# One stream of projection blocks through three stages, with the next stage's first weights prepared ahead

## The reference

```python
proj = xn @ w_in[l]   # [branch gates (3*D) | RWKV-7 cols | S5 cols | Mamba-2 cols (z, xBC, dt)]
o_r = ...             # RWKV-7 time mixing
o_s = ...             # S5: Re(C h) + D u, with the scan h of a diagonal complex state
o_m = ...             # Mamba-2 SSD
merged = sig(g_r)*o_r + sig(g_s)*o_s + sig(g_m)*o_m
out = merged @ w_out[l]
# then cross-attention into 256 memory tokens (keys and values from RMSNorm(mem)), and an MLP
```

## Time and profile before

| | |
|---|---|
| median of 3 runs | 4519.31 us (4514.93 to 4529.73) |
| profiled execution | 4515.67 us |
| its span | 4513.9 us |
| TensorE busy over the span | 4102.0 us (91%) |
| VectorE, ScalarE, GpSimd busy | 2517.0, 1420.3, 222.7 us |

### The profile page before, as it was taken

How to read it: one execution, slowest core, us unless ns; L and a number is a source line. 1 busy time by engine, 2 the same in 40 slices (tenths; PEclk the granted TensorE clock), 3 DMA queues, 4 the chain that set the end, 5 groups by cost and what they waited for, 6 DMA issues and landing times. The chain is left out here.

```text
span 4513.9 us, 84409 instructions
## 1 busy us (share of the span) xinstructions
PE 4102.0 (91%) x35797; PEld 3747.0 (83%) x35797; DVE 2517.0 (56%) x4994; ACT 1420.3 (31%) x2428; POOL 222.7 (5%) x161
## 2 busy tenths in 40 slices
PE   8789999989989999878886999987998899999998
PEld 4779989989978888777885777776977889999997
DVE  3334646431278885258766877765553255444446
ACT  2112222221167553322103444433531252111112
POOL 0000000000001111022110000000001100000000
PEclk9899999989989999988997999998999999999999
DMA  5222222233355554545541100005222221111112
GB/s 186 77 84 83 89 82 88 69 98 112 104 146 142 159 145 123 155 141 163 176 141 40 32 29 31 32 13 174 92 96 89 74 90 61 47 47 47 39 37 77
DMA packets 374261, 418.68 MB, mean 93 GB/s; under 512 B 49162, under 2 KB 315964, under 8 KB 373020
## 3 DMA queue, kind: packets, MB, share of 16 engines
q1 hardware_dynamic: 361599, 368.01, 26.8%
q0 software_dynamic: 7680, 27.97, 2.1%
q10 hardware_dynamic: 4608, 17.30, 1.0%
HBM read 289.10 MB, written 121.77 MB: 91 GB/s over the span
## 5 line engine op out<-in xcount | busy, mean ns | idle before, releaser
L1718 PE MATMUL bank<-sum_x_hi,sum_w_hi 128*128 128x352 f32 x768 | 262.8, 342 | 95.4 <-DVE sum_x_lo L1701 38.0
L210 PE MATMUL bank<-xn_hi,pz_whi 128*128 128x352 f32 (+1 forms) x984 | 328.2, 334 | 21.0 <-DVE pz_wlo L195 14.9
L210 PE MATMUL bank<-xn_hi,pz_wlo 128*128 128x352 f32 (+1 forms) x984 | 319.7, 325 | 0.0
L210 PE MATMUL bank<-xn_lo,pz_whi 128*128 128x352 f32 (+1 forms) x984 | 318.0, 323 | 0.0
L3071 PE MATMUL bank<-bx_hi,bp_whi 128*128 128x384 f32 (+1 forms) x768 | 273.8, 357 | 29.7 <-DVE bx_lo L3129 18.4
L224 ACT ACTIVATE ring<-bank 128x352 f32<-128x352 f32 (+1 forms) x273 | 125.6, 461 | 536.0 <-PE bank L210 535.6
L210 PE MATMUL bank<-xn_hi,pb_whi 128*128 128x352 f32 x816 | 274.9, 337 | 18.9 <-DVE pb_wlo L195 13.0
L210 PE MATMUL bank<-xn_lo,pb_whi 128*128 128x352 f32 x816 | 266.1, 326 | 0.0
L210 PE MATMUL bank<-xn_hi,pb_wlo 128*128 128x352 f32 x816 | 265.2, 325 | 0.0
L1718 PE MATMUL bank<-sum_x_lo,sum_w_hi 128*128 128x352 f32 x768 | 256.5, 334 | 0.0
L1718 PE MATMUL bank<-sum_x_hi,sum_w_lo 128*128 128x352 f32 x768 | 256.3, 334 | 0.0
(11 more groups left out here) (695 smaller groups left out, 12227.7 us busy)
## 6 DMA issues: line engine op xcount, KB each, us to landing
ring<-in_w_in_dram SPq DMA_DIRECT2D x90, 512.0 KB, 4.9
proj_scratch<-ring SPq DMA_DIRECT2D x66, 528.0 KB, 3.0
m_seg<-acum_scratch SPq DMA_DIRECT2D x32, 512.0 KB, 7.0
ring<-in_mlp_w_dram SPq DMA_DIRECT2D x16, 1024.0 KB, 5.6
ring<-in_mlp_w_dram SPq DMA_DIRECT2D x32, 512.0 KB, 3.5
gates_scratch<-ring SPq DMA_DIRECT2D x24, 528.0 KB, 4.7
merged_scratch<-sum_gate ACTq DMA_DIRECT2D x24, 528.0 KB, 5.7
m_raw<-proj_scratch SPq DMA_DIRECT2D x24, 512.0 KB, 5.5
```

The source lines that it names most:

```text
L210: last = self.nc.tensor.matmul(ps[0:n, 0:m], w[:, q, 0:n], self.pair[x][:, q, t0:t0 + m], start=q == 0 and j == 0, stop=q == KD - 1 and j ...
L1718: last = self.nc.tensor.matmul(self.banks[e % n][:, 0:m], w[:, b % 2, q, :], self.pair[x][:, q, t0:t0 + m], start=q == 0 and i == 0, stop= ...
```

## The change

- **One stream.** `Columns` is built once, with 91 blocks and two more after them (`follow`): the first two blocks of the output products' weights. Its semaphores are kept over the stages' ends, and its split buffers (`pw_whi`, `pw_wlo`) live until `Sums` is done, which uses them too; the first half of `S5Input` keeps four of its eight row tiles there. Each stage loads two blocks beyond its own last and splits one. The stage of the S5 input loads the first two.
- **Stores.** A stage other than the last no longer waits for its last blocks' stores; the second stage waits for them at its start.
- **Drains.** `used` is gone in `Columns` and `Sums`: ScalarE waits for the product count. In `S5Input` the last matmul of each row tile counts.
- **S5 input.** The prompt products are stored before the sample product is awaited. The first half's eight loads are issued in `front`; the value store goes behind them.
- **S5 weights.** The two halves of a kernel product are issued alternately, and the second writes partitions 64 to 79.
- **Output products.** Block 0 comes split, block 1's weights come loaded. The first input chunk is loaded and split in two halves, and inputs are loaded before weights.

The core of the diff:

```diff
 class Columns:
...
+    def __init__(self, k, pair, parts, follow, split, banks):
+        self.k, self.nc, self.pair, self.banks = k, k.nc, pair, banks
+        self.blocks = [b for part in parts for b in part]
+        self.edges = [sum(len(part) for part in parts[:i]) for i in range(len(parts) + 1)]
+        self.W = [b[0] for b in self.blocks] + follow
...
         n = 2 * KD * P
...
+    def fetch(self, sp, b):
+        sp.dma_start(self.raw[:, b % 2, :, 0:self.width(b)], self.W[b].rearrange("(t p) n -> p t n", p=P)).then_inc(self.loaded[b % 2], 16)
...
     def load(self, sp):
-        for b, (W, _, _) in enumerate(self.blocks):
+
+        for b in range(self.first + 2, self.last + 2):
             yield self.at(b - 2, 0.2)
-            if b >= 2:
-                sp.wait_ge(self.w_lo, b - 1)
-            sp.dma_start(self.raw[:, b % 2, :, 0:self.width(b)], W.rearrange("(t p) n -> p t n", p=P)).then_inc(self.loaded[b % 2], 16)
+            sp.wait_ge(self.w_lo, b - 1)
+            self.fetch(sp, b)
+
+    def prime_load(self, sp, us, freed, count):
+
+        yield us
+        sp.wait_ge(freed, count)
+        for b in range(2):
+            self.fetch(sp, b)
+
+    def settle(self, sp, b):
...
+        for s in range(2):
+            sp.wait_ge(self.stored[s], 16 * ((b + 1 - s) // 2))
+
+    def settled(self, sp):
+
+        yield -100
+        self.settle(sp, self.first)
 
     def store(self, sp):
-        for b, (_, dst, _) in enumerate(self.blocks):
+        for b in range(self.first, self.last):
             yield self.at(b + 1, 0.4)
             sp.wait_ge(self.off, 3 * (b + 1))
-            sp.dma_start(dst, self.staging[0:self.width(b), b % 2, :]).then_inc(self.stored[b % 2], 16)
...
-            sp.wait_ge(self.stored[s], 16 * ((len(self.blocks) + 1 - s) // 2))
+            sp.dma_start(self.blocks[b][1], self.staging[0:self.width(b), b % 2, :]).then_inc(self.stored[b % 2], 16)
+        if self.last == len(self.blocks):
+            yield self.at(self.last + 2)
+            self.settle(sp, self.last)
 
...
     def high(self, act):
-        for b in range(len(self.blocks)):
-            yield self.at(b - 1, 0.5)
+        for b in range(self.first + 1 if self.first else 0, self.last + 1):
+            yield self.at(b - 1, 0.5) if b else -50
             act.wait_ge(self.loaded[b % 2], 16 * (b // 2 + 1))
             if b >= 2:
-                act.wait_ge(self.used, b - 1)
+                act.wait_ge(self.product, 3 * (b - 1))
             n = self.width(b)
...
@@ -210,11 +245,10 @@
                         last = self.nc.tensor.matmul(ps[0:n, 0:m], w[:, q, 0:n], self.pair[x][:, q, t0:t0 + m],
                                                      start=q == 0 and j == 0, stop=q == KD - 1 and j == 2)
                 last.then_inc(self.product, 1)
-            pe.drain().then_inc(self.used, 1)
 
...
 class S5Input:
...
     def sync(self, sp):
...
-                sp.dma_start(self.raw[:, s, q, :], self.k.w_in[q * P:(q + 1) * P, C_S + s * 512:C_S + (s + 1) * 512]).then_inc(self.loaded[s], 16)
+        for q in range(KD):
...
             yield self.at(s, Q5 + 2)
+            sp.wait_ge(self.off, 9 * s + Q5)
+            sp.dma_start(self.k.u_dram[:, 4 * s:4 * s + 4, :], self.out[:, :].rearrange("p (z n) -> p z n", z=4)).then_inc(self.stored, 16)
             sp.wait_ge(self.off, 9 * (s + 1))
-            sp.dma_start(self.k.u_dram[:, 4 * s:4 * s + 4, :], self.out[:, :].rearrange("p (z n) -> p z n", z=4)).then_inc(self.stored, 16)
...
-                        last = self.nc.tensor.matmul(self.banks[n % 6][0:rows, :], self.pair[x][:, q, at], w[:, q, :],
+                        last = self.nc.tensor.matmul(self.banks[n % 6][0:rows, :], self.pair[x][:, q, at], w[q],
                                                      start=q == 0 and j == 0, stop=q == KD - 1 and j == 2)
-                    if i == Q5 and s == 0:
-                        pe.drain().then_inc(self.freed, 1)
+                    if i == Q5 and s == 0 and q < KD - 1:
+                        last.then_inc(self.freed, 1)
...
                 for q in range(QP):
                     last = nc.tensor.transpose(bank[:, q * P:(q + 1) * P], v.ab[:, ri, q].rearrange("p t c -> p (t c)"), k.ident[:, :])
                 last.then_inc(self.turned, 1)
-            for half in range(2):
-                yield self.at(z, -0.40 + 0.05 * half)
-                pe.wait_ge(self.made_c, z + 1)
-                pe.wait_ge(self.off, 2 * z + 2)
-                if half:
-                    pe.wait_ge(self.kern_off, 2 * z + 1)
-                at = slice(64 * half, 64 * half + 64)
-                for q in range(QP):
-                    for ri in range(2):
-                        last = nc.tensor.matmul(bank[0:GC, q * P:(q + 1) * P], v.bb[at, ri, q0 + q, :],
+            yield self.at(z, -0.40)
+            pe.wait_ge(self.made_c, z + 1)
+            pe.wait_ge(self.off, 2 * z + 2)
+            for q in range(QP):
+                for ri in range(2):
+                    for half in range(2):
+                        at = slice(64 * half, 64 * half + 64)
+                        last = nc.tensor.matmul(bank[64 * half:64 * half + GC, q * P:(q + 1) * P], v.bb[at, ri, q0 + q, :],
                                                 v.ca[at, s, ri, q, 0:8, :].rearrange("p t c -> p (t c)"), start=ri == 0, stop=ri == 1)
-                last.then_inc(self.turned, 1)
+            last.then_inc(self.turned, 2)
 
...
                 act.wait_ge(self.turned, 4 * z + 3 + half)
                 if z and half == 0:
                     act.wait_ge(self.placed[1 - s], 16 * Q5 * ((z + 1) // 2))
-                activation(v.kern[:, half:ZG:2, :], bank[0:GC, :].rearrange("p (q n) -> p q n", q=QP), ACT.Copy).then_inc(self.kern_off, 1)
+                activation(v.kern[:, half:ZG:2, :], bank[64 * half:64 * half + GC, :].rearrange("p (q n) -> p q n", q=QP), ACT.Copy).then_inc(self.kern_off, 1)
...
 
             @block.tensor
...
-            if b >= 2:
-                sp.wait_ge(self.w_lo, b - 1)
-            sp.dma_start(self.raw[:, b % 2, :, :], j.W.rearrange("(t p) n -> p t n", p=P)).then_inc(self.loaded[b % 2], 16)
+            if b < 2:
+                continue
+            yield self.at(b - 2, 0.2)
+            if b >= 3:
+                sp.wait_ge(self.w_lo, b - 2)
+            sp.dma_start(self.raw[:, self.slot(b), :, :], j.W.rearrange("(t p) n -> p t n", p=P)).then_inc(self.loaded[b % 2], 16)
...
-                sp.dma_start(self.xraw[:, e % 2, :, :], src[:, :, t0:t0 + m]).then_inc(self.x_in[e % 2], 16)
+                if e == 0:
+                    sp.dma_start(self.xraw[:, 0, 0:4, :], src[:, 0:4, t0:t0 + m]).then_inc(self.early_in, 16)
+                q0 = 0 if e else 4
+                sp.dma_start(self.xraw[:, e % 2, q0:, :], src[:, q0:, t0:t0 + m]).then_inc(self.x_in[e % 2], 16)
...
             yield self.at(b - 1, 0.5)
-            act.wait_ge(self.loaded[b % 2], 16 * (b // 2 + 1))
-            if b >= 2:
-                act.wait_ge(self.used, b - 1)
...
+            if b == 1:
+                act.wait_ge(self.columns.loaded[s], 16 * ((self.base + 1) // 2 + 1))
+            else:
+                act.wait_ge(self.loaded[b % 2], 16 * (b // 2))
...
@@ -1707,18 +1768,21 @@
             for c, (t0, m) in enumerate(chunks3()):
...
-                    pe.wait_ge(self.w_lo, b + 1)
-                if b == self.first[j.x]:
+                if c == 0 and b:
+                    pe.wait_ge(self.w_lo, b)
+                if e == 0:
+                    pe.wait_ge(self.early_lo, 1)
+                elif b == self.first[j.x]:
...
                 for q in range(KD):
+                    if e == 0 and q == 4:
+                        pe.wait_ge(self.x_lo, 1)
...
-            pe.drain().then_inc(self.used, 1)
 
...
-                weave(sums.weights(sp), sums.load_x(sp), sums.previous(sp), sums.gates(sp))
+                weave(sums.load_x(sp), sums.weights(sp), sums.previous(sp), sums.gates(sp))
...
@@ -4057,12 +4126,16 @@
             W = w["xa_wk" if n < 2 else "xa_wv"][0]
             sp.dma_start(self.raw[:, n % 2, :, :], W[:, (n % 2) * 512:(n % 2 + 1) * 512].rearrange("(t p) n -> p t n", p=P)).then_inc(self.loaded[n % 2], 16)
         for v, name in enumerate(("mem_k_prompt", "mem_v_prompt")):
+            if v:
+                yield self.START[3] + 4
+                sp.wait_ge(self.k_off, 4)
+                sp.dma_start(self.k.key_dram, self.keyT[:, :, :]).then_inc(self.out, 16)
+                sp.wait_ge(self.product, 6)
+                for q in range(KD):
+                    sp.dma_start(self.raw[:, 0, q, :], self.k.w_in[q * P:(q + 1) * P, C_S:C_S + 512]).then_inc(self.k.s5_first, 16)
             yield (self.START[2], self.START[3] + 16)[v] + 2
             sp.wait_ge(self.p_off, 4 * (v + 1))
             sp.dma_start(o[name][0, 0].rearrange("(a p) h d -> p a (h d)", p=P), self.made[v][:, :, :]).then_inc(self.out, 16)
-        yield self.START[3] + 20
```

(35 more changed lines are left out.)

129 lines of the change are left out of this document (77 added, 52 removed).

## The result

The changed kernel takes 4424.15 us (median of 4 runs, 4419.95 to 4426.89), the kernel before 4523.39 us (4514.93 to 4529.73). The ratio is 0.9781, with a 95% interval of 0.9768 to 0.9793: faster by 99 us, where 4434 us was forecast in a range of 4416 to 4466. The two profiled executions lie closer together: 4515.67 and 4426.89, 88.8 us apart, since that of before was 7.7 us under its median and that of after 2.7 us over its own.

The account below looks back on a forecast made before the run. TensorE was taken to bound the three projection stages, with waits limiting the output products. The terms sum to −83.5 us from the profiled 4515.67, that is 4432; with part of the base's 3.6 us, forecast 4434, range 4416 to 4466.

Parts of the forecast that it names:

- Drains: Block ends: removing drains saves 16 us in the first stage, 6 second, 12.5 third, 5 output products, 2.1 S5 input.
- the forecast's 12.5: Third projection stage, 34 block ends: 12.5 us saved by removing drains, reduced from 14.3 for waits on others.
- the first rival: Later stages: TensorE waits for the second stream instead, only the first stage's drain gain remains, 4459 us; chance 0.15.
- the 10 us at which the prediction was to fall: Third stage: the forecast falls if TensorE's waits for VectorE or ScalarE rise by more than 10 us.
- Kernel products: S5 weights: alternating halves lets two passes start in the time of one, saving 14 us, bounds 0 and 15.
- The first stage: First projection stage, 41 blocks: shorter by 30 us, from 16 for drains and 14 for S5 kernel products.
- The front: Memory keys to S5 input: stage opens 8.3 us later, parameters give back 6; net +2.4, bounds −2 and +4.5.
- first S5 product later than 140: Start of the S5 input products: a sign that the prediction is wrong, if the first one starts after 140 us.
- Boundaries: Four stage starts from first projection stage to output products: gaps shorter by 8.4, 8.1, 6.3 and 5.1 us.
- the clock's 2.4 us at the second stage's start: Second stage's start: half clock after the long idle expected to go with the shorter idle, saving 2.4 us.
- the fifth rival: Stage boundaries: something else sets the start, so the four give half of their 30 us, 4449 us; chance 0.09.
- The fourth rival: 255 to 1842 us: near-pauseless TensorE gets a lower clock; 0.053 lower eats all 83 us; chance 0.02.

Follow-up runs that it names:

- a_draininc: The changed kernel with a drain after each projection and output block that increments a semaphore nothing waits on: 4464.84 us, ratio 0.9871.
- b_nodrain: The kernel before, without the drains of projection and output blocks, ScalarE waiting for the product count: 4483.79 us, ratio 0.9907.
- a_drains: The changed kernel with a bare drain, on which nothing waits, after each projection and output block: 4462.13 us, ratio 0.9870.
- a_inrow: The changed kernel with the S5 kernel products in one group, all of half 0 before half 1: 4434.35 us, ratio 0.9809.
- a_turns: a_front with the key store before the value store, S5 parameters ahead of the second half's weights, key transposes as own streams: 4411.56 us, ratio 0.9751.
- a_front: The changed kernel with SyncE issuing the eight weight loads first at the front's end, then value store, then key store: 4416.36 us, ratio 0.9756.
- after_again: The changed kernel run once more, unaltered: 4425.82 us, ratio 0.9778.
- a_apart: The changed kernel with every stage loading and splitting its own first weights and awaiting its own last stores: 4451.15 us, ratio 0.9844.
- a_swap: a_apart with the projection's split weights placed behind the normalised tokens in on-chip memory: 4454.1 us, one execution.

## Why the prediction was right, point by point

**What bounds it.** Right. The stages that were called bound by TensorE gave up 54 us and VectorE's busy time stayed.

**Drains.** Between plain matmuls a drain with its increment costs 0.51 us over the next eight (1.79 in a_draininc, 1.27 in the changed kernel), not the 0.42 of its first gap; the 0.08 behind it the prediction left out. Where other matmuls follow the block it costs less (the gap before L600 is 0.58 with a drain and 0.25 without), for which the prediction had taken 1.2 us off. Over 40 ends b_nodrain gives 16.3, 0.41 each, for the forecast's 16: right, with the two corrections nearly offsetting each other. In the second stage it gives 4.3 for 6, with 3 us more at half clock; in the output products 3.7 for 5.

In the third stage the forecast's 12.5 was too much, and the ledger's 9.6 flatters it: about 3 us of the 9.6 are the matmuls' spacing and about 2 the clock (8.9 us at half clock, against 12.8), neither of them in the forecast. Taken for the clock, the drains alone are worth 3 us there by b_nodrain and 7 by a_drains. The gaps at the block ends did shrink by 8.7 us, but TensorE's waits for VectorE and ScalarE within the stage rose from 13 to 19. That is the first rival, for 5 to 9 of its 25 us, and still under the 10 us at which the prediction was to fall. (Its "first stage's 14" is a slip: the sum has 16 there, which makes that rival 23.5.)

**Kernel products.** Right: 14.7 for 14, and 1.8 more in the transposes behind. The rule that the prediction quotes from the Trainium skill (TensorEngine Tiling (Array Packing), Restrictions and Gotchas), that different row tiles can't access one bank at the same time, would have made it 0. This case's trace does not agree: after's pairs start 0.006 us apart in one bank, and 256 passes take 14.8 us instead of 29.5. a_inrow shows a condition that the prediction did not name: neighbours in the list.

**The first stage: the step that was mis-sized.** Forecast −30, measured −40.4. Drains and kernel products with their transposes account for 33, the remaining 7.7 are the spacing of matmuls: from each projection matmul to the next start it is 489.6 us in b_nodrain and 481.9 in the changed kernel. It is no term of the forecast at all. That buffers change their place was in the diff, and was counted as nothing without a reason. The third stage has a share of it too (0.1607 to 0.1594, 3 us).

**The front.** Right in sign and near in size: the stage opened 9.3 us later for 8.3 (just beyond the 4.8 to 9 that the prediction allowed), the value store took 7.6 us to land, between the 4.1 alone and the 8 behind all loads, and the parameters gave back 6.1 for 6. That their transposes' due time moves nothing was right, and a_turns, which gives them streams of their own, gained 4.9 us over a_front together with the parameters' order. One of the prediction's signs of being wrong came true here: first S5 product later than 140 (140.52, and 139.93 in after_again). It was set too tight: its own bound of +4.5 allows 141.8.

**Boundaries.** The gaps are −9.3, −8.2, −6.5 and −6.6, for −8.4, −8.1, −6.3 and −5.1. All four were sized within 1.5 us. a_apart shows that the stages joined account for 20 of these 31; what is left, by subtraction, is 5.3 for the earlier prompt store and 4.8 for the half input chunk. So the fifth rival, half of the boundaries, falls. What failed is the clock's 2.4 us at the second stage's start: the full clock right after the start did come (from 873.82 the next two start 0.24 and 0.16 later), but soon they are 0.29 apart, the half level:

```profile
874.47 0.49 PE L245 MATMUL bank<-xn_hi,pw_whi 128*128 128x352 f32 x1
874.76 0.49 PE L245 MATMUL bank<-xn_lo,pw_whi 128*128 128x352 f32 x1
```

The stage's time at half clock was 44 us in all, as before (42). The forecast priced one place, and the total has its own scatter. The fourth rival, a lower grant in the gapless stream, found nothing: 1.00, 0.93, 0.99 and 0.91, against 1.00, 0.93, 0.99 and 0.92.

**The sum.** Pieces that gave more than forecast make 13.9 us (10.4 of it the first stage), pieces that gave less 8.7 (third stage 2.9, the start of the second 2.3, its blocks 1.9): 83.5 forecast, 88.7 in the profiles. The other 10 to the medians' 99 are the two executions' places among their runs: the base was taken for 3.6 us low, and lay 6 to 11 below the medians of before in the later comparisons.

## What to carry to other kernels

A drain after a unit of work, even one that nothing waits for, cost here two to three matmul starts (0.41 us on average) on an engine that never waits; let the count on the last matmul do its job, and look at once which second stream then becomes late. Two small matmuls on different row halves took the time of one, when they were neighbours in the list; they wrote different partitions, and no run here shows whether that is needed. When moving loads ahead of a stage's end, ask which store's landing closes the stage: eight loads put ahead of that store opened the next stage 9 us later, and a reorder was worth 13 us more.

## What the runs showed that was not expected

- The place of buffers in on-chip memory changes the pace of matmuls: 70 spacings take 11.34 to 11.38 us with the split weights above the S5 data, 11.22 to 11.23 with them below most of it, 11.13 in most blocks with them beside the tokens. The cause is open.
- A drain's semaphore increment costs 0.04 us over the bare drain.
- The pairing of row halves reaches only a few instructions ahead: in 16 + 16 passes in sequence four pairs form, at the change of half.
- TensorE's time at half clock in an unchanged, gapless stage of 306 us varied from 38 to 51 us between executions of the same code (and 55 to 63 in a_drains, a_draininc, a_apart and a_swap). What the last four have in common was not found.
